# Two units of key pages requested one stage earlier, and a changed order of work on GpSimd and VectorE at the start of the last attention stage

## The reference, cut to what matters

```
q, k = rope(rms(heads(q), qn)), rope(rms(heads(k), kn))          # 8 query heads, 2 key heads, 128 wide
prompt: s = q @ k.T / sqrt(128), keys outside the 256 chosen -> -inf ; y = softmax(s) @ v
sample: the same over 1024 cached keys in pages (8 pages of 128 keys per sequence, page_table) and 4 new ones
y = y * silu(gate) ; out = x + concat(y, memory attention) @ w_out
```

## Time and profile before

| what | value |
| --- | --- |
| median of 3 runs (lowest, highest) | 1876.54 us (1876.25, 1878.46) |
| the profiled execution, its own time | 1876.28 us |
| its span in the trace | 1874.7 us |
| busy, share of span | PE 95%, DVE 52%, ACT 32%, POOL 22% |
| mean granted TensorE clock | 0.978 |

### The profile page before, as it was taken

How to read it: one execution, slowest core, us unless ns; L and a number is a source line. 1 busy time by engine, 2 the same in 40 slices (tenths; PEclk the granted TensorE clock), 3 DMA queues, 4 the chain that set the end, 5 groups by cost and what they waited for, 6 DMA issues and landing times. The chain is left out here.

```text
span 1874.7 us, 26519 instructions
## 1 busy us (share of the span) xinstructions
PE 1780.7 (95%) x9417; PEld 1376.2 (73%) x9417; DVE 978.3 (52%) x2277; ACT 601.6 (32%) x1275; POOL 414.0 (22%) x646
## 2 busy tenths in 40 slices
PE   6999999999999997999899999999999689999999
PEld 5666888777788876887776566887777467777887
DVE  5412643233377665211542467888879665675111
ACT  3110332111022112200321346877745445553010
POOL 4301222000133352100342001221005365330000
PEclk9999999999899999999999999999999889999999
DMA  6434333444355467321322111334433874332331
GB/s 212 127 116 121 117 118 108 148 153 133 118 162 185 149 182 262 150 95 52 113 68 77 46 59 67 99 113 138 142 128 102 262 223 133 118 104 84 108 118 45
DMA packets 134349, 236.97 MB, mean 126 GB/s; under 512 B 28486, under 2 KB 60774, under 8 KB 134218
## 3 DMA queue, kind: packets, MB, share of 16 engines
q1 hardware_dynamic: 110506, 171.96, 28.4%
q0 software_dynamic: 17328, 56.24, 9.5%
q10 hardware_dynamic: 6384, 7.08, 1.1%
HBM read 169.05 MB, written 66.17 MB: 125 GB/s over the span
## 5 line engine op out<-in xcount | busy, mean ns | idle before, releaser
L1212 PE MATMUL layer_acc<-layer_w_hi,layer_xT_hi 128*128 128x512 f32 x640 | 262.2, 410 | 0.2 <-PE all_banks L1360 0.2
L1214 PE MATMUL layer_acc<-layer_w_hi,layer_xT_lo 128*128 128x512 f32 x640 | 253.4, 396 | 0.0
L1213 PE MATMUL layer_acc<-layer_w_lo,layer_xT_hi 128*128 128x512 f32 x640 | 252.9, 395 | 0.0
L2773 PE MATMUL front_acc<-front_w_hi,front_xT_hi 128*128 128x512 f32 x520 | 218.8, 421 | 10.4 <-DVE front_w_lo L3314 4.9
L2774 PE MATMUL front_acc<-front_w_lo,front_xT_hi 128*128 128x512 f32 x520 | 206.9, 398 | 0.0
L2775 PE MATMUL front_acc<-front_w_hi,front_xT_lo 128*128 128x512 f32 x520 | 206.9, 398 | 0.0
L1212 PEld LDWEIGHTS layer_acc<-layer_w_hi,layer_xT_hi 128*128 128x128 f32 x640 | 122.0, 191 | 30.6 <-issue 5.9
L1213 PEld LDWEIGHTS layer_acc<-layer_w_lo,layer_xT_hi 128*128 128x128 f32 x640 | 121.4, 190 | 26.7 <-issue 2.6
L1214 PEld LDWEIGHTS layer_acc<-layer_w_hi,layer_xT_lo 128*128 128x128 f32 x640 | 121.0, 189 | 27.0
L2773 PEld LDWEIGHTS front_acc<-front_w_hi,front_xT_hi 128*128 128x128 f32 x520 | 98.9, 190 | 43.9 <-issue 12.2
L3099 ACT ACTIVATE front_index_rows<-odd_bias,front_candidate 128x1024 bf16<-128x1024 f32 (+3 forms) x128 | 124.9, 982 | 8.6 <-DVEq L3463 5.0
(11 more groups left out here) (675 smaller groups left out, 3594.5 us busy)
## 6 DMA issues: line engine op xcount, KB each, us to landing
all_w<-in_w_even POOLq DMA_DIRECT2D x80, 256.0 KB, 3.6
h_even<-layer_st SPq DMA_DIRECT2D x79, 256.0 KB, 2.2
all_w<-in_w_odd POOLq DMA_DIRECT2D x61, 256.0 KB, 3.6
h_odd<-front_st SPq DMA_DIRECT2D x55, 256.0 KB, 2.0
layer_scratch<-h_even SPq DMA_DIRECT2D x46, 256.0 KB, 3.1
all_scratch<-in_w_mem SPq DMA_DIRECT2D x32, 256.0 KB, 3.9
all_scratch<-h_even SPq DMA_DIRECT2D x32, 256.0 KB, 3.5
all_scratch<-x SPq DMA_DIRECT2D x14, 512.0 KB, 3.6
```

The lines of the kernel that those rows point to most:

```text
L1212: T.matmul(out[0:rows, :], xh[:, kk, to], wh[:, r, :], start=(kk == 0), stop=False)
L1213: T.matmul(out[0:rows, :], xh[:, kk, to], wl[:, r, :], start=False, stop=False)
L1214: ins = T.matmul(out[0:rows, :], xl[:, kk, to], wh[:, r, :], start=False, stop=(kk == KC - 1))
L2773: T.matmul(out[0:rows, :], xh[:, k, to], wh[:, r, :], start=(k == 0), stop=False, skip_group_check=True)
```

## The change

1. **Key units 3 and 4 (indices 2 and 3) are requested in `layer1_front`.** Their 8 pages are loaded by SP in slots 63 and 64, into columns 2640 to 4687 of the tile `index_rows`, which held the cached memory values (`cc`) until the values' products are done (`vmix`). `index_rows` becomes the first tile of the stage, so that its address is that of the big tile of `layer1_back`; the ring's buffers 2 and 3 there move to the same columns, and two of the six buffers of turned keys move out of the way. In `layer1_back`, `load_k(2)`, `load_k(3)` on SP and `load_last_k(2)`, `load_last_k(3)` on POOL are dropped, and PE's `turned(u)` no longer waits for loads where u < 4.
2. As the tiles of `layer1_front` move, **ACT's wait for `c.x1_last`** moves forward, to the small weights in slot 0.
3. **POOL's plan names prep ahead of smp in slots 0 to 5**: the power for tile p = 2 (slot 2) goes ahead of the pages of that slot.
4. **DVE's plan names job ahead of prep in all slots.**
5. For p = 2 DVE's weighting and rotation move to one slot later each (slots 4 and 5), and PE's transposes to slots 6 to 8 (`TURN` 4 to 5).

```
@@ layer1_front
+        Q = s.sb("index_rows", [P, 5 * TOK])
+            def first_keys(u, to, n_pool):
+                for p in range(4):
+                    page = sp.value_load(c.page_ids[0:1, PAGES * u + p:PAGES * u + p + 1], min_val=0, max_val=n_pool - 1)
+                    src = a["cache_attn_k"][0, bass.ds(page, 1)].rearrange("o s h d -> (o s) (h d)")
+                    sp.dma_start(to[p], src).then_inc(kp_in, 16)
...
-                for _ in range(6):
+                yield
+                sp.wait_ge(vmix, NB)
+                for u in (2, 3):
+                    first_keys(u, [Q[:, EARLY_KEYS + 1024 * (u - 2) + 256 * p:EARLY_KEYS + 1024 * (u - 2) + 256 * p + 256] for p in range(4)], n_pool)
+                    yield
+                for _ in range(3):
                     yield
...
-            sp.wait_ge(kp_in, 16 * 8)
+            sp.wait_ge(kp_in, 16 * 16)
@@ ACT, squares()
                 act.wait_ge(small_in, 16)
+                act.wait_ge(c.x1_last, 32)
@@ ACT, copies()
-                act.wait_ge(c.x1_last, 32)
@@
-def back_plan():
+def back_plan(early=(), job_first=False):
     plan = [[] for _ in range(77)]
+    for s in early:
+        plan[s].append("prep")
     for s in range(1, 40):
         plan[s].append("smp")
+    if job_first:
+        for g in range(67):
+            plan[g].append("job")
     for s in range(57):
-        plan[s].append("prep")
-    for g in range(67):
-        plan[g].append("job")
+        if s not in early:
+            plan[s].append("prep")
+    if not job_first:
+        for g in range(67):
+            plan[g].append("job")
@@ layer1_back
-    TURN = {p: 4 if p == 2 else 6 for p in START}
+    TURN = {p: 5 if p == 2 else 6 for p in START}
-        kp = [... WH[:, 1024 * r + 256 * p:1024 * r + 256 * p + 256] ...]
+        kp = [... G[:, EARLY_KEYS + 1024 * (r - 2) + 256 * p:EARLY_KEYS + 1024 * (r - 2) + 256 * p + 256] ...]
@@ SP preps()
                 load_qk(2)
-                load_k(2)
                 load_value(0)
                 load_value(1)
                 sp.dma_start(gc[0], ...)
-                load_k(3)
                 load_qk(3)
@@ POOL preps()
-                load_last_k(2)
-                load_last_k(3)
-            follow(plan, 0, None, prep=preps(), smp=smps(), ...)
+            follow(back_plan(early=range(6)), 0, None, prep=preps(), smp=smps(), ...)
@@ PE turned(u)
-                if u >= 2:
-                    loads = u // KRING + (r >= 2)
+                if u >= KRING:
+                    loads = u // KRING
@@ DVE preps()
                             link(V.tensor_tensor(y, y, bc(ssq[u][0:rows, :], 2, HD), ALU.mult))
+                        if step == 3:
                             for lo, hi, j, n in ((0, QH * HD, 0, QH), (QH * HD, QK, 1, KVH)):
...
-                        if step == 3:
+                        if step == 4:
                             rotate(V, link, y, HD // 8, rt[:, PREP[p]], tmp, rows, H10)
...
-            follow(plan, 0, None, prep=preps(), smp=smps(), ...)
+            follow(back_plan(job_first=True), 0, None, prep=preps(), smp=smps(), ...)
```

More of the change, by code:

```diff
@@ L2272, in front_plan @@
     return plan, amid
+EARLY_KEYS = 2640
 def layer1_front(nc, c, a, o):
@@ L2303, in layer1_front @@
         S = c.scratch
-        Q = s.sb("index_rows", [P, 5 * TOK])
         BF = mybir.dt.bfloat16
@@ L2350, in layer1_front @@
         qTm = S[:, 4096:5120].rearrange("p (h b q) -> p h b q", h=NH, b=NB)
-        cc = [Q[:, 2640 + 1024 * u:3664 + 1024 * u].rearrange("p (m n) -> p m n", m=MC) for u in range(2)]
+        cc = [Q[:, EARLY_KEYS + 1024 * u:EARLY_KEYS + 1024 * u + 1024].rearrange("p (m n) -> p m n", m=MC) for u in range(2)]
         mss, mx, tot = ([s.sb(f"{n}{u}", [P, NH]) for u in range(2)] for n in ("mem_rstd", "mem_max", "mem_total"))
@@ L2553, in loads_qk @@
                 sp.dma_start(c.rope[0:SMP, TILES], a["rope"][SEQ:TOK]).then_inc(qk_par, 16)
-                for _ in range(6):
+                n_pool = a["cache_attn_k"].shape[1]
+                yield
[4 more added lines that the diff above has]
+                for _ in range(3):
                     yield
@@ L2559, in loads_qk @@
                 sp.wait_ge(split_d, UNITS // T1 * KC)
-                n_pool = a["cache_attn_k"].shape[1]
                 for u in range(2):
[L2562 to L2565, removed]
+                    first_keys(u, [c.key_page(u, p) for p in range(4)], n_pool)
                 yield
@@ L3730, in layer1_back @@
         WH, WL = G[:, 0:OUT_CHUNKS * D], G[:, OUT_CHUNKS * D:2 * OUT_CHUNKS * D]
-        kp = [[c.key_page(r, p) if r < 2 else WH[:, 1024 * r + 256 * p:1024 * r + 256 * p + 256] for p in range(4)] for r in range(KRING)]
-        skT = [(WH[:, 4096 + 1024 * u:5120 + 1024 * u] if u < 2 else WL[:, 2048 + 1024 * u:3072 + 1024 * u]).rearrange("p (n k) -> p n k", n=KVH)
+        kp = [[c.key_page(r, p) if r < 2 else G[:, EARLY_KEYS + 1024 * (r - 2) + 256 * p:EARLY_KEYS + 1024 * (r - 2) + 256 * p + 256] for p in range(4)] for r in range(KRING)]
+        skT = [(WH[:, 10624:11648] if u == 0 else WH[:, 5120:6144] if u == 1 else WL[:, 2048 + 1024 * u:3072 + 1024 * u]).rearrange("p (n k) -> p n k", n=KVH)
                for u in range(TRING)]
@@ L4051, in load_slice @@
                 pool.dma_start(raw[w % RAW], a["w_out_odd"][:, k, 512 * half:512 * half + 512]).then_inc(w_in[w % RAW], 16)
-            follow(plan, 0, None, prep=preps(), smp=smps(), job=idle(), ties=idle(), weights=weights(), out=idle())
+            follow(back_plan(early=range(6)), 0, None, prep=preps(), smp=smps(), job=idle(), ties=idle(), weights=weights(), out=idle())
         @block.tensor
@@ L4545, in outputs @@
                     yield
-            follow(plan, 0, None, prep=preps(), smp=smps(), job=jobs(), ties=late_ties(), weights=weights(), out=outputs())
+            follow(back_plan(job_first=True), 0, None, prep=preps(), smp=smps(), job=jobs(), ties=late_ties(), weights=weights(), out=outputs())
 OUTS = [(1, SEQ, D), (NB, NT, D), (1, 1, NH, HD, HD), (1, 1, NH, HD), (1, 1, NH), (1, NB, NH, HD, HD),
```

## The result

The changed kernel takes 1880.2 us against 1876.49 us (medians of 16 runs each): a ratio of 1.0022, 95% interval 1.0015 to 1.0030: slower by 0.2%, a small difference, but clear of the noise. In the profiled executions the span grows by 4.0 us, from 1874.7 to 1878.7. The forecast was 1876.2 us, no measurable change.

A forecast was written before the change was run, and what follows sets the result against it. PE works 95% of the span, so time is won only where it stands or is clocked lower. Terms -3.6 - 0.5 - 0.3 + 1.7 - 0.4 + 2.0 + 0.8 = -0.3 gave 1876.2 us; 8 in 10: 1871.0 to 1880.5.

The forecast's parts named there:

- slot 39 to 44, "net +2.0": Last stage: sums 2.8 us later, w_out slices about 3 us later, rotation ending near 1627.2, wanted at 1625.04: net +2.0 us.
- Slots 12 to 20, "-0.5" and "-0.3": Last stage, slots 15 to 20: job 15's mask no longer waits for sums, -0.5 us; slot 17's select may go free, -0.3.
- The free select: DVE's select of slot 17, held before by POOL's weighting, may go free: -0.3 us.
- Slot 23 to 28, "+1.7": Last stage: sums 3.1 us later, rotation ends at 1570.1, PE wants it at 1568.47: a PE stop of 1.7 us.
- Slots 31 to 36, "-0.4": Last stage: sums 2.3 us later but rotation still in time, 0; the mask wins 0.4 us: -0.4.
- 47 to 52, "+0.8": Last stage: the same lateness as in slots 39 to 44, with more room: +0.8 us.
- The start, "-3.6 at slot 12": Start of the last stage: power 2.4 us sooner, job 3's 0.9 us won, one hold smaller: 3.6 us gained at slot 12.
- third rival: Start of the last stage: DMA engines bound it, so the start gives 1.5 us; 1878.5 us in all, chance 0.12.
- may stay: Start of the last stage: PE's 1.2 us wait for unit 4's pages may stay, but moves 3.0 to 5.6 us earlier.
- The costs put at nothing in front: In layer1_front: eight early pages on SP in slots 63 and 64, and ACT's wait for the x1 stores, cost 0 each.
- second rival: From slot 28 on: GpSimd's chain becomes the bound, late rotations paid, sum +4.9 us, 1881.4 us; chance 0.18.
- The rule as the prediction used it: Shared port: a VectorE instruction with two SBUF inputs and a GpSimd instruction reading SBUF exclude each other for a whole instruction.

The follow-up runs named there:

- experiment 4: The changed kernel, with POOL asking for the first four slices of w_out at the head of slot 39: 1.0003 of the kernel before, 1876.8 us.
- experiment 3: The changed kernel with DVE's old order (row work ahead of the job) in all slots: 0.9982 of the kernel before.
- experiment 8: The changed kernel with DVE's old order in all slots but 39, where the job goes ahead of the row sums: 1.0007 of the kernel before.
- experiment 5: The kernel before with the early pages alone; POOL's power, DVE's job and the turn of tile 2 as before: 0.9972, 1870.4 us.
- experiment 6: The kernel before with one edit, POOL's row work ahead of its pages in slots 0 to 5: 0.9999.
- experiment 10: The kernel before with the early pages alone, plus three small unread requests on POOL at the head of the last stage: 1.0008, 1876.6 us.
- experiment 12: The kernel before with the early pages and POOL's row work ahead of its pages in slots 0 to 5: 0.9978.
- experiment 9: The kernel before with the early pages, plus POOL asking for the first four slices of w_out at the head of slot 39: 0.9988.
- experiment 11: The changed kernel with DVE's old order in all slots but 15, where the job goes ahead of the row sums: 0.9981 of the kernel before.

## Why the prediction was wrong

**The direction failed on one term, slot 39 to 44, "net +2.0".** It measured +4.9 (5.2 - 0.3 in the table), and +4.0 with that slot's exchange alone. The prediction named the late slices, "land about 3 us later; DVE's first split stands at 1621 with the y of the next slot behind it", and then priced the slot by the rotation, 2.2 us late. The rotation was late, but caused no wait, since PE was held longer by something else. What the step left out: the split stands until its slice lands, its cast is then held 1.4 us longer by POOL's weighting (1.85 against 0.41), the y and the mask behind it come only after both instructions of the split, and PE's work behind the stop runs at the lower clock (22.47 us against 20.32). With 4.9 in place of 2.0 the sum is +2.6 us.

**Slots 12 to 20, "-0.5" and "-0.3".** They measured +1.5 from job 11 to 16 and 0 from 16 to 21. The order of slot 15 costs 1.0 us, in all four kernels with the exchange (10.3 us for jobs 13 to 16, against 9.3 or 9.4): PE stands 1.58 us in slot 17 (until 1522.32), as I read it for a copy of DVE that now comes behind the sums and the ties. The other 0.5 us, from job 11 to 13, is small beside the scatter of that stretch (9.2 to 12.1 us over all traces). The free select came: 0.87 us at 1526.57. What it is worth these traces can't tell: the stretch from job 16 to 21 takes 25.1 us before and after, but 22.5 us in experiment 4, whose program is that of the change there, and 23.4 and 25.1 us in experiments 3 and 8, which are alike there too.

**Slot 23 to 28, "+1.7".** Right to a tenth: 22.3 against 20.6 us, by a wait of 1.63 us for the rotation.

**Slots 31 to 36, "-0.4", and 47 to 52, "+0.8".** Measured +0.3 (0.0 at job 28, +0.3 at 38) and +0.4. Both small, the first with the wrong sign.

**The start, "-3.6 at slot 12".** The size held in this trace: -3.2 at job 11, -3.1 at job 12, and DVE's wait shrank from 4.18 to 0.71 us. There is some luck in it: experiment 4, the same program up to slot 39, has -0.6 at job 11, where PE's wait for unit 4's pages was 5.7 us and not 4.0. Its cause was only half right. The prediction booked the three dropped POOL requests to the arrival of unit 4's pages alone, and the 2.4 us sooner power to POOL's new order. Experiments 5, 6, 10 and 12 show that the dropped requests, 1.15 us each on POOL, move the power by 3.1 us by themselves, and that the order adds 0.4. Bytes have little part in it, since experiment 10 leaves all but 24 KB of them out and has no gain. That refutes the third rival's reason for the gain at the start, and its 1.5 us. But something of it holds once DVE puts the job first. Job 3's exponential then starts 5.3 us sooner than with the pages alone (-8.3 against -3.0), PE stands 4.0 us for unit 4's pages and 1.7 us for tile 2's rotation, and at job 11 both kernels are at -3.2. The prediction had this wait at 1.2 us ("may stay") and the later turn of tile 2 at 0. So the job-first order won nothing at the start, as I read the traces, because what PE waits for next does not come sooner with it; no run has the pages of unit 4 earlier still.

**The costs put at nothing in front** (pages on SP, ACT's moved wait) hold as far as can be told: the stage's trace gives experiment 5 -5.5 us, the timed runs -5.3 us, with some 2 us to either side. Job 0's exponential scatters by 9.6 us between executions (1458.47 to 1468.07), but 8.4 us of that are there already at the first product of `layer1_front` (from 892.40 to 900.84 us), up to which the stages are those of the kernel before. From that product to job 0's exponential the three traces with the old front take 566.1 to 567.6 us, the eleven with the new one 566.0 to 568.3 us.

**The second rival** had the size (+4.9, 1881.4 us; 1880.2 measured) and too small a chance, 0.18. But of its lateness "paid in full at slots 28, 44 and 52" only slot 28 was a stop for the rotation. The third rival's time is 1878.3 us by its own terms (2.1 us less gain than the forecast), not 1878.5.

## What to carry to other kernels

When two blocks trade places in an in-order queue, follow everything that the delayed block releases, requests included, to the first instruction that waits for them, and price that wait with all that is queued behind it; here a 3 us delay cost 4 to 5 us through a DMA request, and the obvious consumer, the rotation, added nothing to that. A part of a change that takes requests off a busy engine's queue can carry the gain that another part claims: with the pages alone the kernel is 0.28% faster than before, the lowest ratio of all versions here, and no reordering added to that. An order that brings an engine sooner to its next input wins only if that input comes sooner too: here PE got back from the job-first order a wait for key pages. Work that has its inputs early belongs where the engine would otherwise wait, ahead of work that must wait for its inputs.

## What the runs showed of the hardware

**A request costs POOL the same for 8 KB as for 128 KB.** Each of the three small ones of experiment 10 stands 1.15 us after the other (1463.81, 1464.98, 1466.12), of which some 0.54 are the request and 0.6 the idle time around its register load, as for whole pages. Both have 128 rows; a request with fewer rows was not run.

**PE's clock scatters between executions of the same instructions.** Experiments 5 and 9 run the same program up to slot 39. Behind a wait of 1.42 us for the rotation in slot 12, the four transposes take 0.66 us in one and 1.11 us in the other. From job 11 to 13, pages alone and then pages with slices ahead:

```profile
1508.70:1518.20 9.50, 8.06 (x66) 6.04 (x67) 4.17 (x15) 4.42 (x12) 5.07 (x11) 1.00 0.87 271
```

```profile
1502.50:1514.60 12.10, 10.68 (x65) 7.94 (x66) 4.12 (x15) 4.33 (x11) 6.40 (x13) 0.72 0.81 248
```

That is 2.6 us of difference (2.7 us from exponential to exponential), PE at 2.4 GHz throughout in the first and for the larger part at 1.2 GHz in the second. It makes a difference of up to 3 us between single traces in these slots no measure of an edit, which is how I came to the refuted expectation of experiment 11. The Trainium skill (TensorE: Matmul & The Clock Gate, Part 1: The HAM clock gate) says that the point at which the clock changes differs between executions of one kernel; these two traces agree. What sets it here, no run shows.

**A cast with one SBUF input is held too.** The cast of 512 columns takes 0.41 or 0.42 us in the other 23 casts of this line in the stage after the change, and 1.85 us, or 1.81 us in experiment 8, when it starts inside a weighting instruction of POOL. The Trainium skill (SBUF — State Buffer, Who interferes with whom) counts casts among the VectorE instructions that can take the shared port pair, and lets the first to ask keep it for a whole instruction; both rows agree. The rule as the prediction used it spoke of two SBUF inputs only, and so did not see this one coming.
